# Gate products of four heads in the four quarters of TensorE's rows, instead of one at a time in the first quarter

## The reference, cut to what matters

```
q, k, v, r, a_lr = split_cols(h @ od_w_in, ...)            # a_lr: 16 columns
log_a = log_sigmoid(a_lr @ gla_w_a2 + gla_b_a) / 16        # 16 x 512: four heads of 128
cum   = cumsum(log_a) in each chunk of 64 tokens           # q*exp(cum), k*exp(-cum), ...
```

## Time and profile before

| | |
|---|---|
| median of 3 runs | 1771.84 us (1764.5, 1771.84, 1773.58) |
| profiled execution: its own time | 1775.91 us |
| its span, first to last instruction | 1774.0 us |
| PE busy | 1673.1 us, 94% |
| DVE, ACT, POOL busy | 48%, 35%, 16% |
| slots with gates, 4 to 11 | 889.16 to 953.06 us |

### The profile page before, as it was taken

How to read it: one execution, slowest core, us unless ns; L and a number is a source line. 1 busy time by engine, 2 the same in 40 slices (tenths; PEclk the granted TensorE clock), 3 DMA queues, 4 the chain that set the end, 5 groups by cost and what they waited for, 6 DMA issues and landing times.

```text
span 1774.0 us, 22631 instructions
## 1 busy us (share of the span) xinstructions
PE 1673.1 (94%) x7910; PEld 1346.8 (76%) x7910; DVE 859.3 (48%) x1695; ACT 623.7 (35%) x1567; POOL 280.4 (16%) x500
## 2 busy tenths in 40 slices
PE   3998888999999869999999999999999999979997
PEld 3776666777777658888867888888888888868886
DVE  4767543466667556453343233343434444344443
ACT  4622232467666544332253122222222332131111
POOL 1865000000000161110000022221222211000000
PEclk9999998999999979999999999999999999989999
DMA  8344444445454676322232333333333332184663
GB/s 218 119 136 150 118 131 123 139 147 152 138 153 138 194 206 204 105 96 95 74 106 101 116 109 113 103 113 110 107 119 105 114 103 86 66 256 148 197 193 107
DMA packets 271817, 235.50 MB, mean 133 GB/s; under 512 B 81657, under 2 KB 224825, under 8 KB 271705
## 3 DMA queue, kind: packets, MB, share of 16 engines
q1 hardware_dynamic: 260408, 232.94, 42.1%
q10 hardware_dynamic: 11296, 1.12, 0.5%
HBM read 140.09 MB, written 93.91 MB: 132 GB/s over the span
## 4 chain that ended last, share of the span: by engine, by line
PE 60%; DVE 1%; DMA 1%; SPq 1%; issue 1%; ACT 0%; POOLq 0%; POOL 0%; ACTq 0%; DVEq 0%
PE odd_bank L2127 29%; PE odd_bank L2282 10%; PE odd_bank L2171 9%; PE odd_bank L2152 2%; PE odd_bank L2229 2%; PE odd_bank L2226 1%; PE odd_bank L2227 1%; PE odd_bank L2208 1%; PE odd_bank L2196 1%; PE odd_bank L2185 1%; DVE glu_g_lo L1972 0%; PE odd_bank L2210 0%; PE odd_bank L2136 0%; PE odd_bank L2237 0%; PE odd_bank L2236 0%
## 5 line engine op out<-in xcount | busy, mean ns | idle before, releaser
L2127 PE MATMUL odd_bank<-ht_hi,odd_w_hi 128*128 128x512 f32 x768 | 319.9, 416 | 1.1 <-DVE odd_w_lo L1889 1.1
L2127 PE MATMUL odd_bank<-ht_lo,odd_w_hi 128*128 128x512 f32 x768 | 300.5, 391 | 0.0
L2127 PE MATMUL odd_bank<-ht_hi,odd_w_lo 128*128 128x512 f32 x768 | 299.0, 389 | 0.0
L1185 PE MATMUL ev_acc<-ht_hi,ev_w_hi 128*128 128x512 f32 x576 | 242.5, 421 | 1.5 <-DVE ht_lo L891 1.5
L1185 PE MATMUL ev_acc<-ht_hi,ev_w_lo 128*128 128x512 f32 x576 | 228.7, 397 | 0.0
L1185 PE MATMUL ev_acc<-ht_lo,ev_w_hi 128*128 128x512 f32 x576 | 228.3, 396 | 0.0
L1901 DVE COPY odd_stage<-odd_bank 128x512 f32<-128x512 f32 x96 | 66.4, 691 | 228.2 <-PE odd_bank L2127 228.2
L2127 PEld LDWEIGHTS odd_bank<-ht_hi,odd_w_hi 128*128 128x128 f32 x768 | 144.4, 188 | 40.3 <-issue 7.6
L2127 PEld LDWEIGHTS odd_bank<-ht_lo,odd_w_hi 128*128 128x128 f32 x768 | 144.1, 188 | 32.0
L2127 PEld LDWEIGHTS odd_bank<-ht_hi,odd_w_lo 128*128 128x128 f32 x768 | 144.7, 188 | 27.1
L1185 PEld LDWEIGHTS ev_acc<-ht_hi,ev_w_hi 128*128 128x128 f32 x576 | 110.3, 192 | 30.6 <-issue 4.5
(11 more groups left out here) (286 smaller groups left out, 2943.4 us busy)
## 6 DMA issues: line engine op xcount, KB each, us to landing
odd_gl_in<-scr_heads SPq DMA_DIRECT2D x32, 640.0 KB, 4.2
scr_heads<-odd_stage SPq DMA_DIRECT2D x64, 256.0 KB, 2.0
odd_w_raw<-od_w_in SPq DMA_DIRECT2D x48, 256.0 KB, 3.6
ev_w_raw<-ev_w_in SPq DMA_DIRECT2D x36, 256.0 KB, 4.6
ev_x_tile<-x SPq DMA_DIRECT2D x16, 512.0 KB, 3.8
ev_s_cos_sin<-scr_s_cos_sin SPq DMA_DIRECT2D x32, 256.0 KB
odd_xo_sum<-x SPq DMA_DIRECT2D x16, 512.0 KB, 4.3
scr_x<-odd_xo_sum SPq DMA_DIRECT2D x16, 512.0 KB, 2.8
```

The source lines that it names most:

```text
L1185: mm = pe.matmul(acc[n % 3][:], w[j][:, k, :], h[:, k, t], start=(k == 0 and r == 0), stop=(k == KT - 1 and r == 2))
L2127: mm = pe.matmul(acc[n % 4][:], w[j][:, k, :], h[:, k, t], start=(k == 0 and q == 0), stop=(k == KT - 1 and q == 2))
```

## The change

The four heads' gate products of one block are now issued together, `gates(b)`, after the first half of slots 4, 6, 8 and 10. Each head has 32 rows (partitions) of its own: head h reads rows 32h to 32h + 31 of `low` and of `w2`, and writes a bank of its own (2, 3, 6, 7). For that the low rank values are held four times: `w_low` has 64 columns (upper, lower, upper, lower), the low rank products make 64 rows, and DVE copies these twice, into rows 0 to 63 and 64 to 127 of `low`. `w2` comes in eight DMAs without zeroing, `causal` moves to another place in memory and behind them in SP's queue, and `prm_in` is 176 (eleven DMAs). The gates are taken in the order block by block in place of head by head; which slot treats gate k on ACT, DVE and SP stays. `gates(b)` waits until ACT and DVE have read all gates of block b - 1.

```
-        w_low, low_raw = at("w_low", 76, [P, 352], F32R), at("w_low_raw", 77.5, [P, KT, RANK])
-        causal = at("causal", 78, [P, P])
+        w_low, low_raw = at("w_low", 76, [P, KT, 4 * RANK], F32R), at("w_low_raw", 78, [P, KT, RANK])
+        causal = at("causal", 48, [P, P])
...
-        low, w2 = at("ga_low", 0, [2 * RANK, SEQ]), at("ga_w2", 8, [2 * RANK, GH, DK])
+        low, w2 = at("ga_low", 0, [P, SEQ]), at("ga_w2", 8, [P, DK])
...
-        ps_z = [bank[2][:], bank[3][:]]
+        ps_z = [bank[b][:] for b in (2, 3, 6, 7)]
...
-                sp.dma_start(causal[:], prm["causal"]).then_inc(prm_in, 16)
                 for k in range(3, KT):
                     load_wo(k)
...
                 load_w(1)
-                sp.wait_ge(made, 5)
-                for at_ in (0, RANK):
-                    sp.dma_start(w2[at_:at_ + RANK], prm["gla_w_a2"][0].rearrange("r (h d) -> r h d", h=GH)).then_inc(prm_in, 16)
+                for h in range(GH):
+                    for at_ in (2 * RANK * h, 2 * RANK * h + RANK):
+                        sp.dma_start(w2[at_:at_ + RANK], prm["gla_w_a2"][0][:, h * DK:(h + 1) * DK]).then_inc(prm_in, 16)
+                sp.wait_ge(x1_stored[1], 16 * (NT // 2))
+                sp.wait_ge(hn_done, NT)
+                sp.dma_start(causal[:], prm["causal"]).then_inc(prm_in, 16)
...
                     for k in gates_at(n - 1):
-                        h, b = divmod(k, NB)
+                        b, h = divmod(k, GH)
-                act.wait_ge(low_clear, 1)
-                s.copy(w_low[:, 0:2 * RANK * KT].rearrange("p (k n) -> p k n", k=KT)[:, :, 0:RANK], low_raw[:]).then_inc(low_hi_done, 1)
+                s.copy(w_low[:, :, 0:RANK], low_raw[:])
+                s.copy(w_low[:, :, 2 * RANK:3 * RANK], low_raw[:]).then_inc(low_hi_done, 1)
...
-                    j, h = k % 2, k // NB
+                    j, h = k % 2, k % GH
...
-                    s.activation(ge[:, j], ps_z[j], ACT.Abs, bias=ga_b[:, h:h + 1]).then_inc(abs_done, 1)
+                    s.activation(ge[:, j], ps_z[h], ACT.Abs, bias=ga_b[:, h:h + 1]).then_inc(abs_done, 1)
...
-                act.wait_ge(prm_in, 80)
+                act.wait_ge(prm_in, 176)
-                        v.tensor_copy(low[:, t], acc[n % 4][0:2 * RANK]).then_inc(acc_free, 1)
+                        v.tensor_copy(low[0:4 * RANK, t], acc[n % 4][0:4 * RANK])
+                        v.tensor_copy(low[4 * RANK:P, t], acc[n % 4][0:4 * RANK]).then_inc(acc_free, 1)
...
-                v.memset(w_low.ap().bitcast(F32), 0.0).then_inc(low_clear, 1)
...
+                for r in range(2):
+                    low_part = v.tensor_tensor(w_low[:, :, (2 * r + 1) * RANK:(2 * r + 2) * RANK], low_raw[:],
+                                               w_low.ap().bitcast(F32)[:, :, 2 * r * RANK:(2 * r + 1) * RANK], ALU.subtract)
+                low_part.then_inc(w_ready, 1)
...
-                dve.wait_ge(made, 4)
-                v.memset(w2[:], 0.0).then_inc(made, 1)
-                dve.wait_ge(prm_in, 80)
+                dve.wait_ge(prm_in, 176)
-                            mm = pe.matmul(acc[n][:], w_low[:, 2 * RANK * k:2 * RANK * k + P], h[:, k, cols(b)],
+                            mm = pe.matmul(acc[n][0:4 * RANK], w_low[:, k], h[:, k, cols(b)],
...
-                def gate(k):
-                    h, b = divmod(k, NB)
-                    if k == 0:
-                        pe.wait_ge(prm_in, 80)
+                def gates(b):
+                    if b == 0:
+                        pe.wait_ge(prm_in, 176)
                         pe.wait_ge(acc_free, 4)
-                    if k >= 2:
-                        pe.wait_ge(abs_done, k - 1)
-                        pe.wait_ge(m_done, k - 1)
-                    pe.matmul(ps_z[k % 2], w2[:, h], low[:, b * BLK:(b + 1) * BLK], start=True, stop=True).then_inc(z_ps, 1)
+                    else:
+                        pe.wait_ge(abs_done, 4 * b)
+                        pe.wait_ge(m_done, 4 * b)
+                    for h in range(GH):
+                        rows = slice(2 * RANK * h, 2 * RANK * (h + 1))
+                        pe.matmul(ps_z[h], w2[rows], low[rows, cols(b)], start=True, stop=True).then_inc(z_ps, 1)
...
                     for k in gates_at(n):
-                        if k % 2 == 0:
-                            gate(k)
+                        if k % GH == 0:
+                            gates(k // GH)
                     if is_pair(m + 1):
                         first(m + 1)
                     products(n, KT // 2).then_inc(acc_full, 1)
-                    for k in gates_at(n):
-                        if k % 2 == 1:
-                            gate(k)
```

More of the change, by code:

```diff
@@ L1442, in gates_output_odd @@
         (wo_hi_done, wo_lo_done, o_full, x1_done, osq_done, ovar_done, orstd_done, hn_done, o_turned, to_hi, to_lo, wo_free,
-         low_hi_done, low_clear) = (c.sem("out_" + n) for n in (
+         low_hi_done) = (c.sem("out_" + n) for n in (
             "w_hi_done", "w_lo_done", "full", "x1_done", "sq_done", "var_done", "rstd_done", "normed", "turned", "to_hi", "to_lo",
-            "w_free", "low_hi_done", "low_clear"))
+            "w_free", "low_hi_done"))
         wf_in, mix_in, xf_in, f_stored = c.sems("wf_in", KT), c.sems("mf_in", 2), c.sems("xf_in", 2), c.sems("f_stored", 2)
@@ L1913, in gate_min @@
                         dve.wait_ge(la_stored[j], 16 * (k // 2))
-                    v.tensor_scalar(gm[:, j], ps_z[j], ga_b[:, h:h + 1], 0.0, ALU.add, ALU.min).then_inc(m_done, 1)
+                    v.tensor_scalar(gm[:, j], ps_z[h], ga_b[:, h:h + 1], 0.0, ALU.add, ALU.min).then_inc(m_done, 1)
                 def gate_log(k):
@@ L2035, in _ @@
                 dve.wait_ge(low_hi_done, 1)
-                by_k = lambda ap: ap[:, 0:2 * RANK * KT].rearrange("p (k n) -> p k n", k=KT)
-                v.tensor_tensor(by_k(w_low)[:, :, RANK:2 * RANK], low_raw[:], by_k(w_low.ap().bitcast(F32))[:, :, 0:RANK],
-                                ALU.subtract).then_inc(w_ready, 1)
+                for r in range(2):
+                    low_part = v.tensor_tensor(w_low[:, :, (2 * r + 1) * RANK:(2 * r + 2) * RANK], low_raw[:],
+                                               w_low.ap().bitcast(F32)[:, :, 2 * r * RANK:(2 * r + 1) * RANK], ALU.subtract)
+                low_part.then_inc(w_ready, 1)
                 for m in range(NT):
```

## The result

The change took 1757.12 us (median of four runs, 1753.28 to 1758.27) against 1771.88 us of the kernel before beside it (four runs, 1764.5 to 1773.58). The ratio is 0.992, with a 95% interval of 0.9905 to 0.9934: 11.7 to 16.8 us less. The profiled execution took 1753.28 us, its span 1751.5, against 1774.0 before.

A forecast was written before the change was run, and what follows sets the result against it. PE, busy 94% of the span, was taken to bound the kernel. Gains of 15.2 (gates) and 1.2 (way into slot 4) less 1.4 (new wait) made 15.0 us, taking 1771.84 to 1756.8, say 1757 us; range 1750 to 1766.

The forecast's parts named there:

- Part 1, four gates side by side: On PE, slots 4 to 11: four gates on different rows overlap, a group costs 1.30 us; gain 15.2 us.
- The upper bound, 4.42: Highest price of a group of four gates on PE: four times the two passes plus slower starts once, 4.42 us.
- The estimate by the Trainium skill's figure: Price of a gate group on PE from the skill's measured gain of 3.07: 1.66 us, gain 13.7 us.
- Part 2, the way in: PE's idle time between the low rank products and slot 4, behind the load of `w2`, goes; gain 1.2 us.
- The copies: DVE's six copies of low rank values take 0.63 us each, done at 890.2; `gates(0)` has 0.5 us to spare.
- Part 3, the new wait: `gates(b)` waits for the block before; one 4.0 us store ahead of `gates(2)` loses 1.4 us, bounds nothing to 9.9.
- The edits at no cost: 64-column low products, extra cast and subtraction for `w_low`, early memset and `causal` load: nothing taken, at most 8.3 us.
- The sum: Whole kernel: 15.2 + 1.2 - 1.4 = 15.0 us gained, median 1756.8, say 1757 us.
- rival 1: Gate passes on PE overlap only as a staircase of five steps: group 2.85 us, gain 8.8, time 1763; 8%.
- rival 2: Gate products on PE do not overlap: group 4.42 us, gain 2.5, time 1769; 7%.
- Rival 3: All three later gate groups wait for stores of about 3.8 us: 8.7 us lost, time 1764; 9%.
- Rival 4: Slower than before: gate groups wait for longer stores, deciding from 5.1 us each; 3%.

The follow-up runs named there:

- the kernel with that edit alone: The kernel before, with only the zeroing of `w2` and the wait for it removed; 1765.23 us (one run).
- Four buffers: The change with the log gates in four buffers instead of two, loads of weights left in place; 1754.25 us (one run).
- the repeat: The changed kernel run once more without an edit; 1759.55 us (6 runs), ratio 0.9936 against the kernel before.
- the kernel on one quarter: The change with all four heads on rows 0 to 31, grouped but not side by side; 1764.88 us (10 runs), ratio 0.9976 against the kernel before.

## Why the prediction came out

Predicted were 1757 us, a gain of 15.0, and 1757.12 were measured, a gain of 14.8. By its steps:

**Part 1, four gates side by side: right.** 1.30 us for a group was taken, 1.29 is what it costs; 20.4 - 4 x 1.29 = 15.2, as said. The step no row had shown, from halves to quarters, held: all four run in step. The upper bound, 4.42 for four on the same rows, was too high: there they take 3.87, since the 1.05 counted for each of the four was read from a lone gate, and behind another gate one costs 0.86. The estimate by the Trainium skill's figure came out too high for the same reason. The Trainium skill ("TensorE: Matmul & The Clock Gate", Part 3, Measured speedup vs the span model) gives 3.07 for four quarters of 512 columns. Read as the gain over four on one quarter, which the page does not spell out, the trace agrees with it: 3.87 / 1.29 = 3.0. The estimate of 1.66 came from applying it to four lone gates of 1.274.

**Part 2, the way in: right in cause and size.** 1.2 us was taken, 1.31 went (from 1.53 to 0.22); the kernel with that edit alone shows the same. `causal` was not in the way: it was issued at 869.30, and DVE began its first copy at 874.25 without a wait.

**The copies: a term mis-sized.** 0.63 us each was taken from a group of three 32-row copies, whose records are 0.67 long and start 0.60 apart. The 64-row ones take 0.68, and each starts only behind the one before, 0.70 apart. The last of the eight ended at 881.0, `gates(0)` was due at 880.95 by the distance in slot 6 and began at 881.14, so the 0.5 us to spare were more than gone: slot 4 lost 0.24 us. DVE's timeline has the last pair:

```profile
879.62 0.68 DVE L1899 COPY odd_ga_low<-odd_bank 64x512 f32<-64x512 f32 x1
880.31 0.68 DVE L1900 COPY odd_ga_low<-odd_bank 64x512 f32<-64x512 f32 x1
```

**Part 3, the new wait: right in cause and place, and its size depends on the execution.** One store of 4.0 us ahead of `gates(2)`, behind the load of weights, was the forecast, with 1.4 us lost; the store took 4.1, PE stood 1.80, and slot 8 lost 3.47, since the granted clock fell behind the wait. In the second profile the store took 4.0, PE stood 1.64 and 1.72 went. What the prediction left out is the clock. Four buffers, which leave the store as long as it is, take all of it away: the wait is shown to be the buffer's.

**The edits at no cost: right.** From the first to the last low product it is 15.45 us with 64 columns (862.44 to 877.89) and 15.61 with 128 (872.02 to 887.63 before). The other edits show in no stretch.

**The sum.** From the last low product on, the two profiles of the change show 12.8 and 14.4 us gained, where 15.0 was said; what is missing is slot 8's clock and the copies. The 14.8 between the medians lies closer to the forecast than these terms do, and the medians of the repeat lie only 9.4 apart (its ratio of 0.9936 is 11.3 us, the interval 8.5 to 14.3), with the stage of two lengths mixed in. The mechanism is shown; that the total fell on the forecast to a tenth of a microsecond is chance.

**The rivals.** The staircase (rival 1) asked for groups of 2.85; they are 1.29, and four records stand in the first tenth. The Trainium skill's strict program order (same page, Part 3, What overlaps and what doesn't) spoke for it. The trace does not agree with that rule for products on different rows: the first passes of all four heads start before the second pass of any. Nothing overlapping (rival 2) is the kernel on one quarter, which was run: 3.87 a group, no gain in the slots. Rival 3 wanted three waits and there was one; DVE's wait of 1.45 us in the earlier trace rows, which spoke for it, was for a store of 3.5 us with no load ahead. Rival 4 wanted stores of 5.1 us and none was over 4.2.

**Left open.** Why the stage ahead of the low products has two lengths. Its long form goes with a longer wait of PE in the gated unit (the GLU) for DVE's `glu_g_lo`, and slower products behind it, on PE's timeline of before, of the change and of the change again:

```profile
659.90 0.80 PE L2152 MATMUL odd_bank<-glu_g_hi,ht_hi 128*128 128x512 f32 x1 [4.97 <-DVE glu_g_lo L1972]
```

```profile
651.14 0.50 PE L2153 MATMUL odd_bank<-glu_g_hi,ht_hi 128*128 128x512 f32 x1 [2.56 <-DVE glu_g_lo L1975]
```

```profile
660.05 0.80 PE L2153 MATMUL odd_bank<-glu_g_hi,ht_hi 128*128 128x512 f32 x1 [7.18 <-DVE glu_g_lo L1975]
```

By the three tables above, 4.2 and 5.1 of the 6.2 and 5.6 us that the long form adds are idle PE. In the nine profiles PE's longest wait there is 5.0 to 7.2 us in the four long ones and 1.8 to 2.6 in the five short ones. No experiment touched what makes DVE late there.

## What to carry to other kernels

Products with few rows can share the array if each has rows of its own (here each also had a bank of its own, and nothing else was tried); test on the nearest pair in the trace whether both passes start together, then cost the group at one product's price, and price the serial case by back-to-back products, not by lone ones. When work is gathered into groups, look at the buffers behind it: the group waits for its slowest member's store, and one more pair of buffers was worth more here (0.76 us in the slots) than moving the transfer that slowed the store, which then slowed another store and came later to the engine that needed it. Before a gain is read from two spans, compare stretches that the edit doesn't touch: here one of them differs by 5 to 6 us between executions of the same kernel.

## What the runs showed that I had not expected

The granted clock fell behind 1.80 us of idle PE in one execution and stayed at 1.00 behind 1.64 in another. It also fell with less than 0.1 us of idle PE: on one quarter, where PE is busy nearly all the time, the table by stretches shows slot 4's group of serial 32-row products (886.1 on) and the products behind it.

```profile
886.10:890.00 3.90, 3.85 (x8) 1.55 (x8) 0.75 (x1) 2.62 (x5) 0.00 (x0) 0.84 0.00 0
890.00:895.80 5.80, 5.80 (x14) 4.04 (x13) 0.00 (x0) 1.17 (x2) 0.00 (x0) 0.52 0.00 0
```

A mean of 0.52 over 5.8 us is close to the lower of the two levels (1.2 of 2.4 GHz), and products there start 0.43 apart in place of 0.23. Behind slot 8's group the same came (0.56 from 923.0 to 926.8), behind those of slots 6 and 10 not. So four heads on the same rows are not only three times as long: in two of four groups they cost another 1.6 and 3.1 us by the clock (slot 4's 3.4 less its 0.24 for the copies), which groups on four quarters did only behind the 1.80 us of idle PE.
